# Neighbourhood attention: the second half of the queries projected as feature rows instead of token rows

## The reference

```python
q, k, v, g = jnp.split(h @ w_in, 4, axis=-1)          # h: 256 x 1024, w_in: 1024 x 4096
q = q.reshape(b_, rows, GRID_W, N_HEADS, HEAD_DIM) * HEAD_DIM ** -0.5
kc, vc = jnp.split(hc @ w_in[:, WIDTH:3 * WIDTH], 2, axis=-1)   # 256 context tokens
# scores of each query: 4 rows x 16 columns of its own neighbourhood (+ a table), and all 256 context tokens
p = softmax(concat([s_loc, s_ctx]));  o = p_loc @ v + p_ctx @ vc
y = (o * silu(g)) @ w_out
```

## Time and profile before

| | |
|---|---|
| median of 3 runs | 1821.66 us (1820.48 to 1821.74) |
| the profiled execution | 1821.5 us |
| its span | 1819.7 us |
| granted clock of TensorE | 0.998 of full speed |
| busy: TensorE, its weight loads | 1799.0 us (99%), 1483.2 us (82%) |
| busy: VectorE, ScalarE, GpSimd | 941.8 us (52%), 905.6 us (50%), 1365.3 us (75%) |

### The profile page before, as it was taken

One profiled execution on the slowest core, in us unless ns is written; L12 is line 12 of the kernel. 1 busy time (PEld: TensorE's weight loads), 2 busy tenths in 40 slices (PEclk: granted clock), 3 DMA queues, 4 the chain that ended last, 5 costly groups with the idle time before them and its releaser, 6 DMA issues.

```text
span 1819.7 us, 25066 instructions
## 1 busy us (share of the span) xinstructions
PE 1799.0 (99%) x9322; PEld 1483.2 (82%) x9322; DVE 941.8 (52%) x1755; ACT 905.6 (50%) x1337; POOL 1365.3 (75%) x568
## 2 busy tenths in 40 slices
PE   6999999999999999999999999999999999999999
PEld 5888788877889888887888888888888878888887
DVE  4673766778754524866553230713095865143152
ACT  3324424764455644456554644564445565545452
POOL 2624544559968898977689798969897858888885
PEclk9999999999999999999999999999999999999999
DMA  9853885748776675565466566567655645656663
GB/s 367 295 202 93 277 301 162 197 144 308 243 273 201 211 221 192 178 198 167 134 189 187 182 195 191 194 187 234 193 191 184 190 137 164 192 160 212 189 196 127
DMA packets 200553, 366.61 MB, mean 201 GB/s; under 512 B 32852, under 2 KB 54084, under 8 KB 199876
## 3 DMA queue, kind: packets, MB, share of 16 engines
q1 hardware_dynamic: 197568, 357.52, 62.8%
q10 hardware_dynamic: 2884, 7.73, 1.1%
HBM read 364.12 MB, written 6.13 MB: 203 GB/s over the span
## 4 chain that ended last, share of the span: by engine, by line
PE 98%; DVE 1%; DMA 0%; ACT 0%; ACTq 0%; POOL 0%; issue 0%
PE ps L1247 26%; PE ps L1249 26%; PE ps L1248 26%; PE ps L1373 3%; PE ps L1374 3%; PE ps L1375 3%; PE ps L1938 1%; PE ps L1939 1%; PE ps L1940 1%; PE ps L1295 1%; PE ps L1865 1%; PE ps L1644 1%; PE ps L1615 1%; PE ps L1505 1%; PE ps L1625 1%; PE ps L1910 1%
## 5 line engine op out<-in xcount | busy, mean ns | idle before, releaser
L613 POOL TENSOR_TENSOR w_lo<-raw,w_hi 128x1024 fp32r<-128x1024 f32 x556 | 1346.4, 2457 | 404.4 <-ACT w_hi L651 383.0
L1247 PE MATMUL ps<-w_hi,act_rows_r 128*128 128x512 f32 x2064 | 816.1, 395 | 4.0 <-POOL w_lo L613 3.3
L1249 PE MATMUL ps<-w_hi,act_rows_r 128*128 128x512 f32 x2064 | 805.9, 390 | 0.0
L1248 PE MATMUL ps<-w_lo,act_rows_r 128*128 128x512 f32 x2064 | 805.4, 390 | 0.0
L651 ACT ACTIVATE w_hi<-raw 128x1024 fp32r<-128x1024 f32 x556 | 572.0, 1058 | 370.1 <-DMA raw<-in_ffn_w_up 99.6
L1247 PEld LDWEIGHTS ps<-w_hi,act_rows_r 128*128 128x128 f32 x2064 | 388.4, 188 | 92.0 <-issue 8.8
L1249 PEld LDWEIGHTS ps<-w_hi,act_rows_r 128*128 128x128 f32 x2064 | 388.2, 188 | 81.8
L1248 PEld LDWEIGHTS ps<-w_lo,act_rows_r 128*128 128x128 f32 x2064 | 388.6, 188 | 77.2
L2593 DVE STREAM_TRANSPOSE ps<-proj 32x256 f32<-32x256 f32 (+1 forms) x384 | 166.6, 434 | 6.5
L2574 DVE TENSOR_TENSOR proj<-proj,ps 128x1024 f32<-128x1024 f32 (+1 forms) x18 | 20.4, 1132 | 252.2 <-PE ps L1249 247.8
L1373 PE MATMUL ps<-act_rows_r,w_hi 128*128 128x512 f32 (+1 forms) x288 | 101.4, 352 | 0.0
(11 more groups left out here) (244 smaller groups left out, 1557.1 us busy)
## 6 DMA issues: line engine op xcount, KB each, us to landing
raw<-in_w_in SPq DMA_DIRECT2D x120, 512.0 KB, 3.8
raw<-in_ffn_w_gate SPq DMA_DIRECT2D x88, 512.0 KB, 4.4
raw<-in_ffn_w_up SPq DMA_DIRECT2D x88, 512.0 KB, 4.4
raw<-in_ffn_w_down SPq DMA_DIRECT2D x88, 512.0 KB, 4.2
proj<-in_ada_w SPq DMA_DIRECT2D x39, 512.0 KB, 8.0
pt<-in_ada_w SPq DMA_DIRECT2D x38, 512.0 KB, 6.4
raw<-in_pool_w_in SPq DMA_DIRECT2D x32, 512.0 KB, 8.0
raw<-in_na_w_in SPq DMA_DIRECT2D x32, 512.0 KB, 5.0
```

The lines of the kernel that those rows point to most:

```text
L613: pool.tensor_tensor(w_lo[:, s, :], raw[:, s, :], w_hi[:, s, :].bitcast(F32), ALU.subtract).then_inc(lo_done, 1)
L1247: pe.matmul(o, h, hi, start=start, stop=False)
L1248: pe.matmul(o, h, lo, start=False, stop=False)
L1249: return pe.matmul(o, c, hi, start=False, stop=stop)
```

## The change

The sixth block is made by `feature_block` with one stream: 128 weight columns stationary, the 256 tokens of x moving, 4 feature tiles in banks 2 and 3 (two in each). ScalarE's `na_high(2)` and `na_high(3)` read these banks where the products left them, and VectorE's `low_of_qk` too; they keep their places in the two queues. The late turns go, and the copy of the block to token rows. The low part of turn 3 now counts the block's banks as free (`acc_free`), and unit 12's scores wait for that. Bank 2 is noted as held by the low part of turn 2, which the first values (unit 0) wait for.

```diff
-NA_TURN_BANK = (6, 7, 3, 3)
+NA_TURN_BANK = (6, 7, 2, 3)
 ...
 def na_high(k):
-    act.wait_ge(pe_done, pe_s.count(("tp", "naq", 0, k)))
+    if k in NA_LATE:
+        act.wait_ge(group_used, G0["na_in"] + 24)
+    else:
+        act.wait_ge(pe_done, pe_s.count(("tp", "naq", 0, k)))
 ...
-    pe.wait_ge(acc_free[(b + 3) % 2], reads(b + 3))
-    for k in range(4):
-        weights(g + 20 + k)
-        for t in range(NT):
-            part(5, k, t, bank_of(b + 5, t))
-        if k == 0:
-            pe.wait_ge(ada_read, max(ADA_AT["na_in"].values()) + 1)
-            na_turn(0)
-            na_turn(1)
+    def early_queries():
+        pe.wait_ge(ada_read, max(ADA_AT["na_in"].values()) + 1)
+        na_turn(0)
+        na_turn(1)
+    feature_block("na_in", 5, 1, {0: early_queries})
+    held[2] = (dve_s, ("qk_lo", "na", NA_LATE[0]))
 ...
-                        if i % 4 == 0:
+                        if i == 12:
+                            pe.wait_ge(acc_free[(b + 5) % 2], reads(b + 5))
+                        elif i % 4 == 0:
                             pe.wait_ge(dve_done, dve_s.count(("qk_lo", "na", i // 4)))
 ...
-                    if 1 <= i <= len(NA_LATE):
-                        if i == 1:
-                            pe.wait_ge(acc_free[(b + 5) % 2], reads(b + 5))
-                        na_turn(NA_LATE[i - 1])
 ...
 def low_of_qk(key, k, scale=0.125):
     dve.wait_ge(act_done, act_s.count(("qk_hi", key, k)))
-    dve.scalar_tensor_tensor(...).then_inc(dve_done, dve_s.one(("qk_lo", key, k)))
+    last = dve.scalar_tensor_tensor(...)
+    if k == NA_LATE[-1]:
+        last.then_inc(acc_free[(B0["na_in"] + 5) % 2], 1)
+    else:
+        last.then_inc(dve_done, dve_s.one(("qk_lo", key, k)))
 ...
 for n in range(6):                      # VectorE, na_layer
     if n == 5:
         for k in NA_EARLY:
             low_of_qk("na", k)
+        break
```

More of the change, by code:

```diff
@@ L2180, in low_of_qk @@
                 dve.wait_ge(act_done, act_s.count(("qk_hi", key, k)))
-                dve.scalar_tensor_tensor(out=qk_lo_pair(k), in0=ps[:, NA_TURN_BANK[k], :].rearrange("p (c n) -> p c n", c=2),
-                                         scalar=scale, in1=qk_hi[:, 2 * k:2 * k + 2, :].bitcast(F32), op0=ALU.mult,
-                                         op1=ALU.subtract).then_inc(dve_done, dve_s.one(("qk_lo", key, k)))
+                last = dve.scalar_tensor_tensor(out=qk_lo_pair(k), in0=ps[:, NA_TURN_BANK[k], :].rearrange("p (c n) -> p c n", c=2),
+                                                scalar=scale, in1=qk_hi[:, 2 * k:2 * k + 2, :].bitcast(F32), op0=ALU.mult, op1=ALU.subtract)
+                if k == NA_LATE[-1]:
+                    last.then_inc(acc_free[(B0["na_in"] + 5) % 2], 1)
+                else:
+                    last.then_inc(dve_done, dve_s.one(("qk_lo", key, k)))
             def pair_of(b, s=0):
```

## The result

The changed kernel took 1824.32 us (median of 14 executions, 1821.80 to 1826.23), the kernel before 1820.89 us (14 executions, 1820.19 to 1822.48). The ratio is 1.0015, with a 95% interval of 1.0008 to 1.0022: slower by some 3 us, where +0.27 us was forecast. As a share this is inside the 0.2% that the prediction took for no change; the time itself lies outside its range of 1820.0 to 1823.6 us. The spread is as telling as the median: 4.4 us against 2.3. In what follows I count executions above 1823 us. The changed kernel has 10 of 14 there; the kernel before, over all its executions here and beside the experiments, 1 of 100 (1830.11; one more stands at 1823.00).

What follows compares the result with a forecast made beforehand. TensorE, with work in 1799.0 of 1819.7 us, was taken to bound the kernel. Narrow products +0.63 us less removed turns 0.36 us gave +0.27 us, a median of 1821.9 us, range 1820.0 to 1823.6 us.

Steps and rivals of the forecast that it cites:

- The narrow products: Sixth block of `na_in`: 96 products of 256 columns replace 48 of 512, at 0.1200 us each, costing +0.63 us.
- The weight loads: Sixth block: loads double from 48 to 96, but overlap and are contained in the measured pace, so no further term.
- rival B: Sixth block: 48 extra weight loads stand on the path at 0.19 us each, +9.1 us, giving 1830.4 us; chance 0.04.
- the rule of the Trainium skill told beside it: Weight loads: they overlap products in flight only when the row group differs; here all use the whole array.
- The +0.1 us worked out from the gap: Sixth block: alternative cost of narrow products from the page's N/2.4 + 2.5 ns, making the whole change about 0.3 us gain.
- The turns: Units 1 and 2: removing two late turns gains 0.36 us at scores 3; the second's time becomes a wait.
- The sum: Whole change: +0.63 us for narrow products less 0.36 us for the turns, +0.27 us.
- rival C: Attention loop: a new bank 2 wait or grown bias-chain wait takes the gain back, at worst +0.63, 1822.3 us; chance 0.15.
- D: Later stages: something far away, such as transfers meeting, moves time by 0.2% (3.6 us), either sign; chance 0.04.
- the bias chain: Attention loop: bias transfer and masking before VectorE's addition; start not moved by the edit, unit 4's addition well in time.

Runs made afterwards that it cites:

- e3: Changed kernel with eight transposes that nobody reads put back where the late turns had stood, into bank 7: 1825.70 us, ratio 1.0026.
- e11: e7 with both splits of queries 2 and 3 one unit later on ScalarE and VectorE: 1820.41 us, ratio 0.9998.
- e7: Changed kernel with SP's second table copy, `keep_rel(1)`, sent behind the last bias transfers: 1820.86 us, ratio 1.0000.
- e12: Kernel before with the second table copy moved as in e7: 1821.25 us, ratio 1.0001.
- e2: Kernel before, its sixth block in token rows with each 512-column product split in two, turns and copy kept: 1824.82 us, ratio 1.0030.
- e1: Changed kernel again, unedited: 1823.83 us, ratio 1.0018.
- e10: Kernel before with 80 idle waits (40 instructions) at TensorE's start: 1821.66 us, ratio 1.0006.
- e5: Kernel before with 160 already met waits (80 instructions) at TensorE's start: 1824.72 us, ratio 1.0014.
- e4: Changed kernel with wide token-row products again in the sixth block, no late turns or copy (different output): 1820.68 us, ratio 1.0000.
- e6: Changed kernel with 352 already met waits (176 instructions) at TensorE's start: 1826.90 us, ratio 1.0034.
- e9: Changed kernel with 200 idle waits (100 instructions) at TensorE's start: 1821.83 us, ratio 1.0008.
- e8: Changed kernel, table copy in its old place, VectorE's `gate_scaled(1)` one unit earlier: 1821.00 us, ratio 1.0002.

## Why the prediction was wrong

*The narrow products*: right. +0.57 us for +0.63, and the pace of `p3_in` held (0.120 us). The small rest lies at the seams of the run, which I had counted as unchanged: from the last product to scores 0 were 0.31 us before and are 0.20 now.

*The weight loads*: right, hidden; rival B falls with the pace of 0.120 us, and with it the rule of the Trainium skill told beside it. The +0.1 us worked out from the gap in the Trainium skill, "TensorE: Matmul & The Clock Gate", section "Back-to-back issue gap", doesn't hold either, against +0.57 measured. The Trainium skill gives that gap for an isolated product, and not for a stream of loads and products as here.

*The turns*: right, and by the mechanism given. -0.34 us at scores 3 for -0.36; the second turn's time became a wait on ScalarE's order. e3 put the turns' time back and scores 3 at 9.32 us; e11 took ScalarE's high part away and scores 3 to 8.57.

*The sum*: right where nothing else happens. e7 against e12 are the change with the second table copy out of the way on both sides. The sixth block and the loop up to scores 15 take 12.57 + 61.94 = 74.51 us in the one and 12.00 + 62.23 = 74.23 in the other, +0.28 us. (The medians, 1820.86 and 1821.25, can't show this: the executions of either kernel fall into two groups, in e12 some 1.1 us apart, and an unequal share in them moves a median by more than 0.28. The granted clock parts them. Those of e12 at 1820.24 to 1820.41 us list a mean of 0.999, those at 1821.25 to 1821.77 one of 0.998; in the profile of before the clock is at half, 1.2 GHz, from 22.0 to 28.8 us, in e12's from 23.5 to 26.9, and from the first product to scores 0 are 293.57 us in the one and 292.65 in the other.) The range of the prediction was widened by 0.6 us below and 1.3 above, without a reason for the difference; the result lies above it either way.

*The step that failed* is rival C's bound: "At worst TensorE keeps nothing of the turns: +0.63, 1822.3 us", with the sentence of D that "TensorE waits nowhere long enough". I had named the bias chain, and then priced it only by what the edit takes from it, and read it only where the turns stood, in units 0 to 4. Eight units on, the same chain had VectorE waiting 2.00 us for a mask and TensorE 1.14 us from waiting itself. What the chain can cost is not bounded by what the edit gains: in the profiles with the loss it cost up to 1.35 us at scores 13 (nothing in e2, 0.65 in e1, 1.35 in e3) and, where the collision came, 2.25 to 2.44 us more at the turned probabilities behind, 3.7 us of waits together in e3. That is the size of the median's 3 us. "TensorE waits nowhere" was true of the profiled execution and said nothing of how close a wait was. e10 adds what no term had either, 3.4 us at half the granted clock behind the wait.

*What was missing from the list* is that the edit moves TensorE's code. I counted instructions by their time, never by their number. e5 shows that 80 more instructions that do nothing bring the loss (+3.6 us in the median, by the interval of the ratio 0.5 to 4.7), and the range had no term for it. As for how the place of the code reaches the mask, this much is in the traces: an instruction queue sends packets of 16 KB on the DMA engines, which the bias transfers use too. There are 65 in before, e4 and e12 and 66 in all the others, and their times move with the number of TensorE's instructions in front; I take them for the fetches of its code. Such a packet appears in the profiles at these times from scores 0, nearest to the bias of the seventh pair (which is issued at 38 to 46 us before, to 48 in e3):

```
before 42.5 and 49.8     after 46.5     e4 44.8 and 50.7     e6 37.3 and 49.5     e9 46.4 and 53.2
e1 47.6   e2 47.2   e3 47.1   e8 47.2   e10 48.6   e5 47.3
```

From the issue of the table copy to the end of the mask went 15.2 to 15.6 us in the profiles of the first line and 16.1 to 16.3 in those of the second, with e5 (15.29 us; its profiled execution was a good one, 1820.37 us) as the exception. (In e7, e11 and e12 the copy goes elsewhere.) That is a correlation over eleven profiles, seen after the fact, and after and e1, the same kernel, stand on either side of it. That a fetch holds up one of the bias packets was argued from it, not shown: the trace does not say which of the 16 DMA engines carries which packet. In e3 a second part came in: SP's queue reached the copy itself 1.7 us later (37.6 us from scores 0, 35.9 before), because issues of the bias in front took longer. Why one kernel has the loss in 7 of 11 executions and not in the other 4 stays open too. What is shown is that instructions which do nothing, at TensorE's start, suffice (e5), that taking the copy out of the chain removes the loss (e7, none of 11), and that the collision of VectorE with GpSimd carries most of it (e8, none of 11).

## What to carry to other kernels

A trace in which the bound engine never waits says nothing of how near it is to waiting. Follow each chain that feeds it (transfer, mask, addition) over all its rounds, and write down the smallest slack, not that of the round where the edit stands; another engine's wait of 2 us on a transfer is the sign. And an edit of a few tens of instructions on a long instruction stream can move its time by more than its own operations do (e5: 80 instructions that do nothing, +3.6 us): where a chain has a microsecond of slack, keep a term of a few us for it, or first take the slow transfer out of the chain, as e7 does, and then judge the edit.

## What the runs showed of the hardware

- An instruction of VectorE with two operands in the on-chip memory (128x256, 0.41 us) took 2.58 to 2.60 us where GpSimd started a 128x1024 one just before, in e2, e3 and e10.
- Two waits on a semaphore that is long satisfied left one TensorE record in the traces (160 waits 80, 352 waits 176). With 352 of them the first product came at 19.9 us, with none to 200 between 10.7 and 11.7.
- A copy of 1.5 MB from memory to memory ahead of eight small-packet transfers on the same queue stretched their issue from 5.5 us (e7) to 7.7 (before) and 9.0 (e3).
- In a wait of 2.4 us TensorE's granted clock fell to half for 3.4 us in e10 and stayed full in e3. The same products took 1.5 us longer in e10.
- Narrow products cost the same fixed part in both orientations, weights stationary or tokens: the block grew by 0.57 us in either (after, e2).
